# A token-wise LayerNorm ahead of the expert router, closed by matmuls, in a two-layer decoder step

## What is computed

```python
x = layer_norm(ALPHA * x + m, ln1_g[l], ln1_b[l])      # m: the mixer's output
logits = (xt @ router).astype(jnp.float32)             # 8 columns
top_vals, top_idx = lax.top_k(logits, TOP_K)
gates = jax.nn.softmax(top_vals, axis=-1)
y = sum over e of combine[:, e:e+1] * swiglu(xt, w_gate[e], w_up[e], w_down[e])
x = layer_norm(ALPHA * x + y, ln2_g[l], ln2_b[l])
```

## Time and profile before

| | |
|---|---|
| median of three runs | 1478.27 us |
| the profiled execution's own time | 1477.94 us |
| its span | 1476.1 us |
| granted TensorE clock, mean of the span | 0.985 |
| TensorE, VectorE, ScalarE, GpSimd busy | 95%, 90%, 75%, 8% |
| moved by DMA | 464.86 MB, mean 315 GB/s |
| the chain that ended last | PE 55%, DVE 33%, issue 5%, DMA 5%, ACT 2% |

### The profile page before, as it was taken

How to read it: one execution, slowest core, us unless ns; L and a number is a source line. 1 busy time by engine, 2 the same in 40 slices (tenths; PEclk the granted TensorE clock), 3 DMA queues, 4 the chain that set the end, 5 groups by cost and what they waited for, 6 DMA issues and landing times.

```text
span 1476.1 us, 39851 instructions
## 1 busy us (share of the span) xinstructions
PE 1396.1 (95%) x17532; PEld 1150.7 (78%) x17532; DVE 1334.9 (90%) x1351; ACT 1112.9 (75%) x1070; POOL 125.0 (8%) x162
## 2 busy tenths in 40 slices
PE   9999999999999999899999999999999889898786
PEld 7778888888887887788777888787886766766663
DVE  3999999555699999899999999999999999999997
ACT  4697766544478775778888878988887987888884
POOL 2411024000162002100000000000000000000001
PEclk9999999999999999999999999999999999899998
DMA  9645466556464438899999999999999999999993
GB/s 315 248 163 167 162 240 207 192 196 224 151 239 145 164 135 328 318 357 391 411 405 396 411 405 402 411 405 400 410 406 412 411 407 411 410 399 410 411 398 125
DMA packets 141349, 464.86 MB, mean 315 GB/s; under 512 B 8235, under 2 KB 10411, under 8 KB 126801
## 3 DMA queue, kind: packets, MB, share of 16 engines
q1 hardware_dynamic: 138960, 457.21, 81.2%
q0 software_dynamic: 1920, 4.55, 1.0%
q10 hardware_dynamic: 288, 0.48, 0.1%
HBM read 460.79 MB, written 2.89 MB: 314 GB/s over the span
## 4 chain that ended last, share of the span: by engine, by line
PE 55%; DVE 33%; issue 5%; DMA 5%; ACT 2%; SPq 0%; DVEq 0%; ACTq 0%
PE ps L886 17%; PE ps L887 16%; PE ps L888 16%; DVE w_lo L2419 14%; DVE w_lo L2422 6%; DVE w_lo L1841 2%; PE ps L995 2%; ACT w_hi L1750 2%; DMA x<-in_moe_w_gate 2%; DMA stage<-in_w_in 1%; DMA stage<-in_moe_w_up 1%; DVE arena L1989 1%; DVE arena L2000 1%; DVE arena L2437 1%; DVE arena L2457 1%
## 5 line engine op out<-in xcount | busy, mean ns | idle before, releaser
L886 PE MATMUL ps<-arena,w_hi 128*128 128x128 f16 (+8 forms) x4016 | 585.5, 215 | 15.9 <-issue 13.3
L888 PE MATMUL ps<-arena,w_lo 128*128 128x128 f16 (+8 forms) x4016 | 585.3, 215 | 12.9 <-issue 12.9
L887 PE MATMUL ps<-arena,w_hi 128*128 128x128 f16 (+8 forms) x4016 | 585.2, 215 | 7.1 <-issue 7.1
L888 PEld LDWEIGHTS ps<-arena,w_lo 128*128 128x128 f16 x4016 | 394.1, 99 | 26.0 <-issue 19.5
L886 PEld LDWEIGHTS ps<-arena,w_hi 128*128 128x128 f16 x4016 | 394.2, 99 | 20.8 <-issue 10.6
L887 PEld LDWEIGHTS ps<-arena,w_hi 128*128 128x128 f16 x4016 | 394.4, 99 | 18.9 <-issue 9.6
L886 PE MATMUL ps<-xhl,w_hi 128*128 128x264 f16 x1024 | 282.6, 276 | 5.4 <-ACT z L1561 2.0
L888 PE MATMUL ps<-xhl,w_lo 128*128 128x264 f16 x1024 | 282.6, 276 | 0.0
L887 PE MATMUL ps<-xhl,w_hi 128*128 128x264 f16 x1024 | 282.6, 276 | 0.0
L1841 DVE SCALAR_TENSOR_TENSOR w_lo<-stage,w_hi 128x2048 f16<-128x2048 f32 (+1 forms) x94 | 208.9, 2246 | 67.8 <-ACT w_hi L1400 67.7
L2419 DVE SCALAR_TENSOR_TENSOR w_lo<-stage,w_hi 128x2048 f16<-128x2048 f32 x92 | 208.4, 2285 | 13.0 <-ACT w_hi L1750 12.9
(11 more groups left out here) (349 smaller groups left out, 1985.5 us busy)
## 6 DMA issues: line engine op xcount, KB each, us to landing
stage<-in_moe_w_up SPq DMA_DIRECT2D x64, 1024.0 KB, 14.5
...
```

Source lines behind the costliest of these rows:

```text
L886: mm(out, ah, bh, start=start, stop=False, skip_group_check=True)
L887: mm(out, ah, bl, start=False, stop=False, skip_group_check=True)
L888: return mm(out, al, bh, start=False, stop=stop, skip_group_check=True)
```

## The change

The norm ahead of the router is no longer applied feature by feature. ScalarE writes the residual sum times gain (`zg`, unscaled) into `x`; TensorE turns its tiles to token rows with transposes that accumulate in PSUM, and multiplies them by the router's columns with the tokens as stationary operand, so that the logits come by token. What is missing is of rank two: minus the mean times the gain, plus the deviation times the bias. Both go in by one closing matmul per bank, with the rows `s_rows` (minus mean, deviation, each as high and low part, on partitions 0, 32, 64 and 96) against `gb_rows` (gain and bias) or `cd_rows` (their sums with the router's columns). The reciprocal deviation is applied by token afterwards, as a scale when the rows are split. The sorting works on unscaled logits.

For this, earlier in layer 1: GpSimd multiplies the router by gain and bias (`gain_rt`), eight matmuls sum them over features (`cd_sums`), GpSimd loads the rows of gain and bias over 64 and 33 partitions, ScalarE and GpSimd split them. The residual for the experts is no longer prepared in `z`: in visit two the scatter's bank starts with the token rows themselves (times 64, `unit_ws`), gates are divided by ALPHA, and VectorE copies instead of adding the first time. Piece PRE+3 is split by VectorE after the token rows, the high halves of PRE+4 and PRE+5 after the gates' sigmoids. Loads m = 16 and 17 wait for other events. `keep_busy` before the logits is gone.

```diff
@@ -712,10 +731,10 @@
                 elif 12 <= m < 11 + TWICE:
                     sp.wait_ge(S["lo_done"], split(PRE + m - 12 + 1))
                 elif m == 11 + TWICE:
+                    sp.wait_ge(S["s_split"], 1)
+                elif m == 12 + TWICE:
                     filled(sp, "logits")
-                elif m == 12 + TWICE:
                     filled(sp, ("xtok", 2, 1))
-                    sp.wait_ge(S["z_start"], KT)
...
+                    pool.wait_ge(S["packed"], 8 * L)
+                    for a, b, name in ((0, 64, "ln1_g"), (64, ROWS, "ln1_b")):
+                        pool.dma_start(gb_land[a:b, :], A[name][1, :].partition_broadcast(b - a)).then_inc(S["gb_ld"], 16)
                 read_out(pool, ("so", l))
...
-                norm(2 * l, [("mix", l, 14 + j // 4, j % 4) for j in range(KT)], l, "ln1_b")
                 if l == 1:
-
-                    pool.wait_ge(S["nz_ready"], 3 * KT)
+                    G.memset(s_rows[0:ROWS, :], 0.0).then_inc(S["s_zero"], 1)
+                    pool.wait_ge(S["mg_split"], 2 * KT)
                     for what in (xtl[:, 2, :], xth[:, 2, :]):
                         G.memset(what, 0.0).then_inc(S["rows_zeroed"], 1)
-                    for j in range(KT):
-                        pool.wait_ge(S["norm_ready"], j + 1)
-                        G.tensor_scalar(z[:, j, :], x[:, j, :], WS * ALPHA, 0.0, ALU.mult, ALU.add
-                                        ).then_inc(S["z_start"], 1)
+                    pool.wait_ge(S["gb_hi"], 1)
+                    pool.wait_ge(S["rows_zeroed"], 2)
+                    G.tensor_tensor(gb_rows[0:2, :], gb_land[0:2, :], gb_rows[0:2, :], ALU.subtract).then_inc(S["gb_lo"], 1)
+                    pool.wait_ge(S["gb_lo"], 1)
+                    G.tensor_tensor(gb_rows[64:66, :], gb_land[64:66, :], gb_rows[64:66, :], ALU.subtract
+                                    ).then_inc(S["gb_lo"], 1)
...
+                    if s == 6 and l:
+                        pe.wait_ge(S["cols_ready"], 2)
+                        for k in range(KT):
+                            t = mm(cd_sums, ones_d[:, :], gain_rt[:, k], start=(k == 0), stop=(k == KT - 1))
+                        t.then_inc(S["cd_full"], 1)
...
-            pe.wait_ge(S["ld_small"], 16 * 11)
-            empty(pe, "logits_t")
-            keep_busy(bank("logits_t"), NORM_IDLE - 3)
-
-            for k in range(KT):
-                pe.wait_ge(S["norm_ready"], k + 1)
-                t = mm(bank("logits_t")[0:NE, 0:T], w_rt[:, k, :], x[:, k, :], start=(k == 0), stop=(k == KT - 1))
-            t.then_inc(full_of("logits_t"), 1)
-
             def token_rows(k):
                 for i in range(3):
                     n = P if i < 2 else NS_
                     name = ("xtok", i, k // 4)
                     if k % 4 == 0:
                         empty(pe, name)
-                    t = nc.tensor.transpose(bank(name)[0:n, k % 4 * P:(k % 4 + 1) * P], x[:, k, i * P:i * P + n], ident)
-                    if k % 4 == 3:
-                        t.then_inc(full_of(name), 1)
...
-            token_rows(0)
-            token_rows(1)
-            read_out(pe, "logits_t")
+                    mm(bank(name)[0:n, k % 4 * P:(k % 4 + 1) * P], x[:, k, i * P:i * P + n], ident, start=(k % 4 == 0),
+                       stop=False, is_transpose=True, skip_group_check=True)
+
+            for k in range(4):
+                pe.wait_ge(S["zg_rows"], k + 1)
+                token_rows(k)
+            stats(2, OUT)
+            pe.wait_ge(S["zg_rows"], KT)
             empty(pe, "logits")
+            lgt = bank("logits")
             for i in range(3):
                 n = P if i < 2 else NS_
-                t = nc.tensor.transpose(bank("logits")[0:n, i * NE:(i + 1) * NE], logit_rows[:, i * P:i * P + n],
-                                        ident[0:NE, 0:NE])
+                for k in range(KT):
+                    mm(lgt[0:n, i * NE:(i + 1) * NE], x[:, k, i * P:i * P + n], w_rt[:, k, :], start=(i + k == 0), stop=False,
+                       skip_group_check=True)
+            pe.wait_ge(S["s_split"], 1)
+            pe.wait_ge(S["cd_rows_ready"], 1)
+            pe.wait_ge(S["cd_top"], 2)
+            for i in range(3):
+                n = P if i < 2 else NS_
+                s_tok = s_rows[0:ROWS, i * P:i * P + n]
+                mm(lgt[0:n, 3 * NE + i:3 * NE + i + 1], s_tok, cd_rows[0:ROWS, NE:NE + 1], start=False, stop=True,
+                   skip_group_check=True)
+                t = mm(lgt[0:n, i * NE:(i + 1) * NE], s_tok, cd_rows[0:ROWS, 0:NE], start=False, stop=True,
+                       skip_group_check=True)
             t.then_inc(full_of("logits"), 1)
-            for k in range(2, KT):
+            for k in range(4, KT):
                 token_rows(k)
+            pe.wait_ge(S["gb_ready"], 2)
+            for h in range(2):
+                for i in range(3):
+                    n = P if i < 2 else NS_
+                    name = ("xtok", i, h)
+                    mm(bank(name)[0:n, :], s_rows[0:ROWS, i * P:i * P + n], gb_rows[0:ROWS, h * 512:(h + 1) * 512],
+                       start=False, stop=True, skip_group_check=True).then_inc(full_of(name), 1)
...
+                    if first:
+                        pe.wait_ge(S["unit_ready"], 1)
+                        for i in range(3):
+                            n = P if i < 2 else NS_
+                            for k, part in enumerate((xth, xtl)):
+                                mm(ps[:, b, i * P:i * P + n], part[0:n, i, d * P:(d + 1) * P], unit_ws[0:n, 0:n],
+                                   start=(i + k == 0), stop=False, skip_group_check=True)
+                    mm(ps[:, b, 0:T], yh[0:cap, d * P:(d + 1) * P], onehot_t[0:cap, :], start=not first, stop=False,
+                       skip_group_check=True)
                     mm(ps[:, b, 0:T], yl[0:cap, d * P:(d + 1) * P], onehot_t[0:cap, :], start=False,
-                       stop=True).then_inc(bank_full[b], 1)
+                       stop=True, skip_group_check=True).then_inc(bank_full[b], 1)
...
+            def norm_by_token():
+                mean = ("mean", 2)
+                filled(act, mean)
+                fn(stat[:, 0, :], bank(mean)[:, 0:T], ACT.Square).then_inc(S["m2_ready"], 1)
+                act.wait_ge(S["s_zero"], 1)
+                fn(s_rows[0:33, :], bank(mean)[0:33, 0:T], ACT.Copy, scale=-1.0).then_inc(S["s_hi"], 1)
+                act.wait_ge(S["var_ready"], 3)
+                fn(stat[64:ROWS, 2, :], stat[64:ROWS, 1, :], ACT.Sqrt).then_inc(S["std_ready"], 1)
+                act.wait_ge(S["std_ready"], 3)
+                fn(s_rows[64:ROWS, :], stat[64:ROWS, 2, :], ACT.Copy).then_inc(S["s_hi"], 1)
+                fn(tri16, tri, ACT.Copy).then_inc(S["tri_ready"], 1)
+                for h in range(2):
+                    for i in range(3):
+                        n = P if i < 2 else NS_
+                        if i == 2:
+                            act.wait_ge(S["rows_zeroed"], 2)
+                        if i + h == 0:
+                            act.wait_ge(S["rs_ready"], 1)
+                        name = ("xtok", i, h)
+                        filled(act, name)
+                        fn(xth[0:n, i, h * 512:(h + 1) * 512], bank(name)[0:n, :], ACT.Copy, scale=rs_tok[0:n, i:i + 1]
+                           ).then_inc(S["xt_hi"], 1)
+                act.wait_ge(S["gd_ready"], 1)
+                fn(route1[:, 4, :], route1[:, 3, :], ACT.Sigmoid)
+                fn(route1[:, 5, :], route1[:, 3, :], ACT.Sigmoid, scale=-1.0).then_inc(S["gs_ready"], 1)
+                filled(act, "ranks")
+                fn(unit_ws, ident16[:, :], ACT.Copy, scale=WS).then_inc(S["unit_ready"], 1)
+                for n in (PRE + AHEAD - 1, PRE + AHEAD):
+                    hi(n)
+
+            def top_rows():
+                for a in (0, 64):
+                    fn(gb_rows[a:a + 1, :], gb_land[a:a + 1, :], ACT.Copy).then_inc(S["gb_ready"], 1)
...
+                            else:
+                                fn(x[:, d, :], z[:, d, :], ACT.Copy, scale=vec_d("ln1_g", 1, d)).then_inc(S["zg_rows"], 1)
+                        if l and s == 14:
+                            act.wait_ge(S["cd_lo"], 2)
+                            for a, of in ((0, slice(0, NE)), (64, slice(NE, 2 * NE))):
+                                fn(cd_rows[a:a + 1, 0:NE], cd_all[a:a + 1, of], ACT.Copy).then_inc(S["cd_top"], 1)
+                            act.wait_ge(S["gb_lo"], 2)
+                            top_rows()
+                if l:
+                    norm_by_token()
...
+            def norm_by_token():
+                mean, msq = ("mean", 2), ("msq", 2)
+                filled(dve, msq)
+                dve.wait_ge(S["m2_ready"], 3)
+                V.tensor_tensor(stat[:, 1, :], bank(msq)[:, 0:T], stat[:, 0, :], ALU.subtract).then_inc(free_of(msq), 1)
+                read_out(dve, msq)
```

(34 more changed lines are left out.)

133 lines of the change are left out of this document (76 added, 57 removed).

## The result

The changed kernel takes 1480.67 us (median of 15 runs, 1478.72 to 1484.13), the kernel before 1477.57 (15 runs, 1474.83 to 1478.95). The ratio is 1.0024 with an interval of 1.0017 to 1.0031: slower, where 2.1 us less had been forecast. The profiled execution took 1479.27 us, its span is 1477.5.

The account below looks back on a forecast made before the run. Taken as the bound: weights' last landing, delayed by the ring's 7.4 us idle before 640 us around the router. Gains 3.2 - 0.65 - 0.4 = 2.1 us took 1477.94 to 1475.8, on the median 1476.2; range 1472.4 to 1481.5.

Parts of the forecast that it names:

- its own signs: Wrong if subtractions end after 583.5, first expert matmul falls outside 605 to 609, or its shift and last landing's differ over 1 us.
- Before the router: Eight small FP32 matmuls between gate projection and first branch cost 0.4 us, bounds 0 to 2.0; ScalarE's and GpSimd's copies nothing.
- GpSimd's subtractions: Two 2x1024 subtractions ahead of the statistics, 2.3 us each from 576.8, ending at 581.4; bounds 579.1 to 594.5.
- the 0.6 us: Running sums waiting for GpSimd's subtractions cost 0.6 us in all, so ScalarE starts the one-partition rows at 582.0.
- The path to the second moment: ScalarE's rows, high half and squares, then GpSimd's sums: last square 588.3 to 588.7, second moment closed at 589.7, 2.7 us gained.
- Logits: Router matmuls by token after the second moment take 4.9 us, to 594.6; bounds 3 to 6.5.
- Sorting to the first expert matmul: Sorting at 595.6, token splits end at 603.8, first expert matmul at 606.7; gain 2.55 us, moving piece 3's split costing 0.65.
- Hidden: ScalarE's high halves 4 and 5 run from 600.8 to 604.8, first gathered copy then to 605.4, costing nothing.
- Visit two at nothing: 48 more short matmuls and a copy for an addition, 1.3 us per half, fit a gap; bound 2.6 us of loss.
- Does it reach the end: Whether the router's gain reaches the last landing: DMA must make up 4.3 us, against 5.9 us of slack; enough, barely.
- The rivals: Fast, gather at 2.4 GHz: 1473.3, chance 0.25; starved ring, gain lost: 1478.2, chance 0.15; slower, held-up statistics: 1489.3, chance 0.15.
- The slower one: Rival: GpSimd's two subtractions hold up the statistics, ending at 594.5, 13 us later; time 1489.3 us; chance 0.15.

Follow-up runs that it names:

- e1: Changed kernel with the PSUM banks of the output projection put back as before the change: 1483.50 us, ratio 1.0044 to the kernel before.
- e2: Kernel before with only the two lines that turn the PSUM banks by four ahead of layer 1's output projection: 1483.58 us, ratio 1.0046.
- e8: e6 with the changed kernel's bank plan again (output projection in banks 4 to 7, then 0 to 3): 1479.22 us, ratio 1.0016 to the kernel before.
- e7: e1 without GpSimd's two 2x1024 subtractions, low parts of gain and bias rows left out: 1480.09 us, ratio 1.0022 to the kernel before.
- e6: Changed kernel with banks put back and subtractions, one-partition rows, ScalarE's PRE+3 high half and VectorE's PRE+3 split reordered: 1472.94 us, ratio 0.9975 to before.
- e5: e1 with 15 filling matmuls between TensorE's mean and second-moment matmuls: 1481.28 us, ratio 1.0029 to the kernel before.

## Why the prediction was wrong

Two steps failed, and each hid part of the other: the banks ahead of the router, counted at nothing, and the path through the second moment to the logits, counted to 589.7 and 594.6. With the banks as the prediction had them (e1) the router's matmuls run from 593.30 to 600.6 and the kernel takes 1483.50 us, not 1476.2, so the second step was wrong without the first. By its own signs the forecast was wrong too: the first expert matmul, 611.26, lies outside 605 to 609. It is 4.6 us behind the 606.7 of the working, 3.0 of them up to the sorting and 1.6 behind it.

- **"Before the router"**: 0.4 us were counted, for the eight small matmuls. They cost nothing: the packed rows' turn on TensorE stood at 561.45 where it had been at 561.60. The two lines on the banks were not counted at all, and this is the first step that failed. In the changed kernel the last residual addition is 6.8 us late; alone they put it off by 7.4 us in the kernel before (e2) and 6.6 in the reordered one (e8), and cost 6.6 and 6.3 us of time.
- **GpSimd's subtractions**: they ended at 581.39, as reckoned (581.4), though from 575.12 on and one of them in 4.06 us. The rule cited from the Trainium skill ("SBUF — State Buffer", section "Who interferes with whom") held, but was applied to the running sums alone. VectorE's two 2x8 additions ahead of them have two SBUF inputs as well, and whichever comes second waits: 2.27 us against 0.34 (e7). By that rule the residual additions, which read PSUM, are free of it, and the trace agrees (0.45 each in e1, beside the second subtraction). The term of the sum that this makes wrong is the 0.6 us: ScalarE's rows start at 584.31 in e1 and at 581.88 without the subtractions (e7), so the subtractions hold them up by 2.4 us.
- **The path to the second moment**: the last square was forecast at 588.3, measured 591.71; VectorE takes the moment up at 593.90, not 589.7. In the changed kernel the banks set that. With the banks put back (e1) both were late too, the last square at 590.57 and the moment at 593.60, since the rows, the high half and the squares stand in one row on ScalarE behind the late additions. This is the second step that failed: GpSimd's last sum ends at 591.41 instead of 588.75, and the wait of 3.46 us for it takes the clock, which the working kept at 2.4 GHz. Only with the order changed (e6) does the chain beat the forecast: last square at 585.09, sorting at 593.89 against 595.6.
- **Logits**: 4.9 us forecast, 4.12 measured at 2.4 GHz, 7.32 at 1.2 (e1). The bound of 6.5 for one stretch at the halved clock was too low.
- **Sorting to the first expert matmul**: 11.1 us forecast, 12.7 measured. 0.65 for the moved split was right in kind (608.29, ahead of the copies at 610.49). What was left out are the six closing matmuls of 512 columns and a turn of four tiles: 2.39 and 2.51 us between logits and ranks, so that the first rank matmul starts at 603.07, 2 us after the mask (601.1). "Hidden" was wrong of ScalarE's gathered copies: its token rows wait for the closing matmuls, the two high halves run from 606.15 instead of 600.8, the copies start at 610.04, and TensorE waits 1.47 us. VectorE's first gathered copy ends near 611.1 as well (610.49 and half of 1.27), so without ScalarE's lateness TensorE would have had its second operand hardly sooner.
- **Visit two at nothing**: right to within 0.2 us. VectorE takes the first half at 749.44 instead of 747.00, 2.4 us later, the shift of 2.2 that was there before; the last piece is 2.2 later.
- **Does it reach the end**: the shift of the first matmul, from -4.7 to +6.6 us, arrives at the last piece to within 0.6 us in ten of the eleven changed kernels of the table; in e5 the piece is 1.6 us later than that. The step was right for the change. DMA pauses were forecast near 600 to 607; there were two, in 585 to 590 (share 0.10: m = 10 and 11 wait for the projection and the second moment) and 605 to 610 (0.16: m = 15 waits for piece PRE+3).
- **The rivals**: none was it. The slower one had the right sign and stage, with the subtractions as its cause; its test (they end after 583.5) came out negative. The subtractions do hold up the statistics, though not by their own end but by way of VectorE's additions, and for 2 to 3 us, not 13 (e7 against e1).

The time itself, 1480.67, is within the range given, and that is luck: its sign and cause are not those forecast, and without the turned banks, as the prediction had reckoned, it would have been 1483.50 (e1), outside the range of 1472.4 to 1481.5.

Left open: why in e5 the last piece is 1.6 us later than the first matmul's shift gives. Whether the banks could be turned without cost by merging the branch's columns in another order was not tried.
